# The first modulation of a conditioned decoder block: one sum over 2048 columns, or four groups of 512, and the first products in quarters

## The reference, cut to what matters

```python
def rms_norm(x, g):
    y = x * lax.rsqrt(jnp.mean(x * x, axis=-1, keepdims=True) + EPS)
    return y * g
def modulate(h, shift, scale):
    return h * (1.0 + scale[:, None, :]) + shift[:, None, :]

cond = jax.nn.silu(c)                        # c: (1, 1024)
mod = cond @ w_ada[0] + b_ada[0]             # w_ada: (1024, 9 * 1024)
sh1, sc1, gt1, sh2, sc2, gt2, sh3, sc3, gt3 = jnp.split(mod, 9, axis=-1)
h = modulate(rms_norm(x, g_ffn1), sh1, sc1)  # x: (1, 1024 tokens, 1024)
x = x + 0.5 * gt1 * ((silu(h @ w1_a) * (h @ w3_a)) @ w2_a)     # d_ff = 2816
# ... then a token-mixing layer, a second SwiGLU block, a last rms_norm
```

## Time and profile before

| | |
|---|---|
| median of 3 runs | 2172.11 us (2169.89 to 2172.18) |
| the profiled execution, own time | 2172.18 us |
| its span | 2170.4 us |
| TensorE busy | 2112.2 us, 97% of the span |
| VectorE, ScalarE, GpSimd busy | 1208.2, 697.0, 1256.6 us |
| mean granted TensorE clock | 0.99 of full |

### The profile page before, as it was taken

How to read it: one execution, slowest core, us unless ns; L and a number is a source line. 1 busy time by engine, 2 the same in 40 slices (tenths; PEclk the granted TensorE clock), 3 DMA queues, 4 the chain that set the end, 5 groups by cost and what they waited for, 6 DMA issues and landing times.

```text
span 2170.4 us, 27323 instructions
## 1 busy us (share of the span) xinstructions
PE 2112.2 (97%) x9650; PEld 1735.7 (80%) x9650; DVE 1208.2 (56%) x1293; ACT 697.0 (32%) x1086; POOL 1256.6 (58%) x876
## 2 busy tenths in 40 slices
PE   7999999999999999999999999999999999999998
PEld 5788888888887778787778778887888888888887
DVE  6865445363556787877875753338532333333246
ACT  5633231313223453332332420116321313232234
POOL 1565563737455367867877765544763737464560
PEclk8999999999999999999999999999999999999999
DMA  8132424151421332232335444311111212112111
GB/s 292 59 117 71 143 69 146 58 174 40 139 73 44 122 97 93 79 103 84 97 79 159 144 161 152 107 48 39 49 57 32 59 58 58 58 39 68 32 56 78
DMA packets 228940, 197.04 MB, mean 91 GB/s; under 512 B 17028, under 2 KB 201520, under 8 KB 227696
## 3 DMA queue, kind: packets, MB, share of 16 engines
q1 hardware_dynamic: 204208, 154.42, 23.0%
q10 hardware_dynamic: 24640, 41.40, 5.9%
HBM read 169.45 MB, written 25.17 MB: 90 GB/s over the span
## 4 chain that ended last, share of the span: by engine, by line
PE 83%; DVE 6%; POOL 3%; ACT 2%; DMA 2%; issue 2%; ACTq 1%; SPq 0%; POOLq 0%; DVEq 0%
PE unit_b L1324 10%; PE unit_d L1324 10%; PE unit_c L1118 9%; PE unit_d L1118 9%; PE unit_c L1324 8%; PE unit_a L1324 7%; PE unit_b L1050 7%; PE unit_a L1050 4%; PE unit_a L930 3%; PE unit_b L930 3%; PE unit_c L930 2%; PE unit_d L930 2%; POOL w_low L812 2%; DMA ada_first<-in_w_ada 1%; PE unit_c L1344 1%
## 5 line engine op out<-in xcount | busy, mean ns | idle before, releaser
L861 POOL TENSOR_TENSOR w_low<-raw,w_high 128x512 fp32r<-128x512 f32 x200 | 273.5, 1368 | 214.6 <-ACT w_high L1663 199.1
L831 POOL TENSOR_TENSOR w_low<-raw,w_high 128x512 fp32r<-128x512 f32 x96 | 141.0, 1471 | 287.0 <-ACT w_high L1620 287.0
L1663 ACT ACTIVATE w_high<-raw 128x512 fp32r<-128x512 f32 x200 | 126.5, 632 | 399.8 <-PE unit_b L1324 140.7
L812 POOL TENSOR_TENSOR w_low<-raw,w_high 128x512 fp32r<-128x512 f32 x100 | 152.7, 1527 | 87.6 <-ACT w_high L1845 81.6
L861 POOL TENSOR_TENSOR w_low<-w_mixed,w_high 128x512 fp32r<-128x512 f32 x80 | 107.2, 1340 | 66.2 <-ACT w_high L1663 61.0
L2452 DVE TENSOR_TENSOR fg_two<-fg_one,unit_b 128x512 f32<-128x512 f32 x60 | 41.2, 687 | 168.0 <-PE unit_b L1324 167.8
L779 POOL TENSOR_TENSOR w_high<-raw,ones 128x512 fp32r<-128x512 f32 x44 | 63.0, 1431 | 94.9 <-PE unit_b L930 30.5
L1620 ACT ACTIVATE w_high<-raw 128x512 fp32r<-128x512 f32 x96 | 60.1, 628 | 172.3 <-PE unit_c L1118 67.1
L1845 ACT ACTIVATE w_high<-raw 128x512 fp32r<-128x512 f32 x100 | 61.3, 628 | 151.0 <-PE unit_b L1050 76.9
L2452 DVE TENSOR_TENSOR fg_one<-fg_one,unit_d 128x512 f32<-128x512 f32 x80 | 54.7, 684 | 94.4 <-PE unit_d L1324 94.4
L1050 PE MATMUL unit_b<-t_high,w_high 128*128 128x512 f32 x240 | 94.1, 392 | 6.7 <-POOL w_low L812 6.7
(11 more groups left out here) (530 smaller groups left out, 6152.6 us busy)
## 6 DMA issues: line engine op xcount, KB each, us to landing
raw<-in_w_a SPq DMA_DIRECT2D x66, 512.0 KB, 4.6
raw<-in_w_b SPq DMA_DIRECT2D x66, 512.0 KB, 3.9
raw<-in_w_in SPq DMA_DIRECT2D x44, 512.0 KB, 3.9
ada_ring<-in_w_ada SPq DMA_DIRECT2D x84, 256.0 KB, 3.7
ada_first<-in_w_ada SPq DMA_DIRECT2D x8, 1024.0 KB, 20.9
sg_kept<-s ACTq DMA_DIRECT2D x16, 512.0 KB, 2.7
s<-sg_kept ACTq DMA_DIRECT2D x16, 512.0 KB, 3.4
ada_ring_last<-in_w_ada SPq DMA_DIRECT2D x28, 256.0 KB, 3.5
```

The source lines that it names most:

```text
L812: pool.tensor_tensor(low_, mixer_plain(q, slots), high.bitcast(F32), ALU.subtract).then_inc(mixer.operand_low, 1)
L831: pool.tensor_tensor(low_, plain, high.bitcast(F32), ALU.subtract).then_inc(f.operand_low, 1)
L861: pool.tensor_tensor(low_, weight_plain(PRODUCTS[q][0], slots), high.bitcast(F32), ALU.subtract).then_inc(f.operand_low, 1)
L1663: act.activation(operand((RING[n] + q) % 4)[0], weight_plain(PRODUCTS[q][0], slots), ACT.Copy).then_inc(f.operand_high, 1)
```

## The change

`w_ada`'s first 2048 columns are now taken in four groups (`MOD_GROUPS`), each with the 256 columns of the shift and the 256 of the scale that belong to two channel tiles. Each group is loaded in two halves of the contraction, by two DMAs each (so 16 DMAs of 512 KB with 1 KB in a row). The first tiles of w1 and w3 are loaded between groups 1 and 2. VectorE sums contraction tiles 0 to 6 of a group (512 columns); tile 7 goes to TensorE, which adds it in the products of one column each (`mod_columns`, 4 columns with 2 products each in a group). Groups 0 and 1 are summed before the first reciprocal, groups 2 and 3 between the steps of the norm, two operations after each of the first seven `low`. TensorE makes columns of groups 0 and 1 between the sums of squares of the first and the second half of the tokens, those of groups 2 and 3 before its steps 4 and 8.

The norm and the first two tiles' products go by quarters: step = 4 * quarter + channel tile, with the quarters (first half of the tokens, tiles 0 to 3), (second half, 0 to 3), (first half, 4 to 7), (second half, 4 to 7). The second reciprocal comes after `low(1)` instead of `low(4)`. ScalarE takes the second root before step 4 of its norm instead of ahead of the norm, and its squares start when all of x is copied. ScalarE's waits for `first_mod` stand before steps 0, 2, 8 and 10.

```diff
-FIRST_MOD = ((0, 2), (2, KD))
+MOD_GROUPS = 4
+BY_VECTOR = KD - 1
+BY_PE = tuple(range(BY_VECTOR, KD))
...
         def normed(n, step):
-            return divmod(step, KD)
+            if n > 0:
+                return divmod(step, KD)
+            quarter, k = divmod(step, HK)
+            return quarter % 2, HK * (quarter // 2) + k
...
-            for k in range(KD):
-                sp.dma_start(ada_first[:, k, :], ada[:, k, 0:16 * P]).then_inc(ada_loaded[k], 16)
-            for r, w in enumerate((a["w1_a"][0], a["w3_a"][0])):
-                sp.dma_start(raw[:, r, :, :], ...)
+            for g in range(MOD_GROUPS):
+                for z in range(2):
+                    for kind in range(2):
+                        first = KD * P * kind + 2 * P * g
+                        sp.dma_start(ada_first[g][:, HK * z:HK * z + HK, kind, :],
+                                     ada[:, HK * z:HK * z + HK, first:first + 2 * P]).then_inc(ada_loaded[2 * g + z], 16)
+                if g == 1:
+                    for r, w in enumerate((a["w1_a"][0], a["w3_a"][0])):
+                        sp.dma_start(raw[:, r, :, :], ...)
...
-            take(A_, 1)
-            for half in range(2):
-                for m in range(KD): ... sums of squares ...
+            def mod_columns(g):
+                pe.wait_ge(ada_summed, g + 1)
+                for n in range(4):
+                    tile = slice((n % 2) * P, (n % 2) * P + P)
+                    to = unit[D_][:, HALF * (g % 2) + 4 * g + n:HALF * (g % 2) + 4 * g + n + 1]
+                    last = pe.matmul(to, ada_first_sum[:, g, n * P:n * P + P], ones[:, 0:1], start=True, stop=not BY_PE)
+                    for k in BY_PE:
+                        last = pe.matmul(to, ada_first[g][:, k, n // 2, tile], cond[:, k:k + 1], start=False,
+                                         stop=k == BY_PE[-1])
+                last.then_inc(ada_full, 1)
+
+            take(A_, 1)
+            square_sums(0)
+            take(D_, J // 2)
+            mod_columns(0)
+            mod_columns(1)
+            square_sums(1)
...
-                for half in range(2):
+                for step in range(2 * KD):
+                    half, k = normed(2 * f.n, step)
...
+                    if f.n == 0 and step in (4, 8):
+                        mod_columns(step // 4 + 1)
+                    pe.wait_ge(h_ready, h0 + step + 1)
...
-                    if n > 0 and step == 6:
+                    if step == (4 if n == 0 else 6):
                         root(1)
...
+            def ada_columns(g, k):
+                if k % HK == 0:
+                    dve.wait_ge(ada_loaded[2 * g + k // HK], 32)
+                to = ada_first_sum[:, g, :]
+                from_ = ada_first[g][:, k, :, :].rearrange("p s n -> p (s n)")
+                if k == 0:
+                    last = dve.tensor_scalar(to, from_, cond[:, k:k + 1], None, mul)
+                else:
+                    last = dve.scalar_tensor_tensor(out=to, in0=from_, scalar=cond[:, k:k + 1], in1=to, op0=mul, op1=add)
+                if k == BY_VECTOR - 1:
+                    last.then_inc(ada_summed, 1)
+                else:
+                    own.then(last)
 
             dve.wait_ge(cond_ready, 1)
-            ada_columns(ada_first_sum, ada_first, 16 * P, ada_loaded)
+            for g in range(2):
+                for k in range(BY_VECTOR):
+                    ada_columns(g, k)
             root(0, 0)
...
+            later_columns = [(g, k) for g in (2, 3) for k in range(BY_VECTOR)]
...
-                    if n == 0 and step == 0:
-                        first_mod(0)
+                    if n == 0 and step < 2:
+                        first_mod(step)
                 for step in range(2 * KD):
                     low(step)
...
-                    if step == 1 and n == 0:
-                        first_mod(1)
-                        dve.sem_inc(unit_free[D_], 1)
-                    if step + ahead == KD:
+                    if n == 0:
+                        for g, k in later_columns[2 * step:2 * step + 2]:
+                            ada_columns(g, k)
+                        if step in (5, 8):
+                            first_mod((step + 1) // 3)
+                        if step == 8:
+                            dve.sem_inc(unit_free[D_], 1)
+                    if step + ahead == (HK if n == 0 else KD):
                         root(n, 1)
                     if step + ahead < 2 * KD:
                         scaled(step + ahead)
```

More of the change, by code:

```diff
@@ L312, in block_kernel @@
         x_rows = sb("x_rows", [P, J, D], rH)
-        ada_first = sb("ada_first", [P, KD, 16 * P], rM)
-        ada_first_sum = sb("ada_first_sum", [P, 16 * P], rH + 56 * KB)
+        ada_first = [sb(f"ada_first{g}", [P, KD, 2, 2 * P], rM + 16 * KB * (MOD_GROUPS - 1 - g)) for g in range(MOD_GROUPS)]
+        ada_first_sum = sb("ada_first_sum", [P, MOD_GROUPS, 4 * P], rH + 32 * KB)
         sq = sb("sq", [P, KD, HALF], rA)
@@ L960, in _, with square_sums @@
                 last.then_inc(setup_full, 1)
-            take(A_, 1)
-            for half in range(2):
+            def square_sums(half):
                 for m in range(KD):
@@ L980, in statistics @@
                 pe.matmul(unit[u][:, t], ones[:, :], s0[:, t], start=False, stop=True).then_inc(stat_full, 1)
[L982 to L988, removed]
             def mixer_whole(here, between):
@@ L1545, in _ @@
                     own.then(load_sqrt())
+            for half in range(2):
+                t = slice(HALF * half, HALF * half + HALF)
                 act.wait_ge(unit_free[C_], 2 * half + 2)
@@ L1565, in norm @@
                 if n == 0:
-                    root(1)
                     for o in range(4):
@@ L1582, in norm @@
                     act.wait_ge(xr_done, 2 * KD * n + step + 1)
-                    for part, (k0, _) in enumerate(FIRST_MOD):
-                        if n == 0 and step == k0:
-                            act.wait_ge(mod_done, part + 1)
+                    if n == 0 and half == 0 and m % 2 == 0:
+                        act.wait_ge(mod_done, m // 2 + 1)
                     own.then(act.activation(tile, tile, ACT.Identity, scale=scale[n][:, m:m + 1],
@@ L2154, in derive_scale, with first_mod @@
                                                 in1=vt[:, GN[n] + k0:GN[n] + k1], op0=add, op1=mul)
[L2156 to L2160 removed]
+            later_columns = [(g, k) for g in (2, 3) for k in range(BY_VECTOR)]
+            def first_mod(g):
+                k0, k1 = 2 * g, 2 * g + 2
+                dve.wait_ge(ada_full, g + 1)
+                for n, first in enumerate((SH[0], SC[0])):
                     a0, a1 = first + k0, first + k1
[L2162 to L2163 removed]
+                    at_ = HALF * (g % 2) + 4 * g + 2 * n
+                    own.then(dve.tensor_tensor(mod[:, a0:a1], unit[D_][:, at_:at_ + 2], vt[:, B_ADA + a0:B_ADA + a1], add))
                 derive_scale(0, k0, k1).then_inc(mod_done, 1)
[L2165 removed]
+                dve.wait_ge(mod_done, g + 1)
             def norm(n, h0, end=None, sums=None):
```

67 lines of the change are left out of this document (19 added, 48 removed).

## The result

| | before | after |
|---|---|---|
| median | 2166.14 us (2162.02 to 2172.18, 12 runs) | 2170.23 us (2165.86 to 2178.06, 12 runs) |
| the profiled execution, own time and span | 2172.18, 2170.4 us | 2178.06, 2176.2 us |
| TensorE busy | 2112.2 us | 2117.1 us |

The ratio is 1.0022, 95% interval [1.0012, 1.0033]: 4.8 us slower, between 2.6 and 7.1 (the two medians alone are 4.1 apart). The forecast was 4.9 us slower. But it set this on 2172.18 us, and the kernel before is at 2166.14 when it is measured twelve times; its first three runs lay high. So the 2177.1 us forecast lies 6.9 us above the measured median.

The account below looks back on a forecast made before the run. VectorE, up to the norm's end at 71.4 us, was the bound. Earlier start -8.9, sums in the loop +11.7, stand for columns +2.4, rest -0.3: 2172.18 + 4.9 = 2177.1 us; range 2169 to 2184.

Parts of the forecast that it names:

- The base: Whole kernel: the profiled execution's own 2172.18 us, 0.07 above the median, to which the change of +4.9 us was added.
- Arrival: Loads of the groups: a group's half in 3.0 us at 347 GB/s, landing at 18.9, 21.9, 24.9 and 27.9.
- Sums ahead: VectorE before the first reciprocal: 0.87 us a sum, reciprocal at 30.7 instead of 39.57, a gain of 8.9 us.
- The rival of cheaper sums: VectorE's sums at 0.75 us each, or a shorter stand: +2 us or so, 2174.3 us; chance 0.24.
- the 1.3 us that the prediction set aside for it: Group 1's last sums on VectorE: one could wait for a GpSimd operation, adding up to 1.3 us to the sum.
- Lead in: VectorE from first reciprocal to first `low`: 30.7 + 3.39 + 0.6 + 1.63 + 0.6 + 0.71 + 0.6 = 38.2 us.
- The thin cover: TensorE's second-half sums of squares end at 41 to 42, ScalarE's second root due at 42.5; any lateness is on the path.
- The loop: VectorE's norm steps 0 to 6: 2.94 us each, 11.7 us of sums in them, step 7 begins at 62.4.
- The wait of `first_mod(3)`: VectorE behind `low(8)`: stands 2.4 us, from 64.2 to 66.6, until TensorE has made the last columns.
- The tail: Norm steps 10 to 15 at ScalarE's pace: last low part at 76.3 against 71.4, TensorE's part ends at about 78.
- near 111 of more than 2.3 us: Sign that the forecast is right: TensorE's stand behind the first tiles, now at 106.33 and 2.31 us long, later and longer.
- all behind the norm moves by 4.9: VectorE's later sums, low parts and ring hang on the norm's end and were to move by 4.9 us.

Follow-up runs that it names:

- after_again: The changed kernel once more with no edit, for a second profile; ratio to the kernel before 1.0018.
- sq_split: Against the changed kernel, TensorE makes half of the second half's sums of squares ahead of group 1's columns; ratio to the kernel before 1.0020.
- cols_early: Against the changed kernel, TensorE makes the columns of group 3 before its step 7 instead of step 8; ratio to the kernel before 1.0013.
- split_early: Against the changed kernel, both TensorE moves: second squares split around group 1's columns, group 3's columns before step 7; ratio to the kernel before 1.0005.

## Why the prediction was right or wrong

The direction was right, and the mechanism in its kind: VectorE's sums in the loop take more than the earlier start gives. The size agrees in part by luck, and the absolute time was wrong, because of the base it was added to. The 0.2% taken as the bound between same and slower lies inside the measured interval, so which of the two it is stays undecided by that bound, though slower than before at all is sure.

- **The base, the step that failed.** "The profiled execution's own time is 2172.18, 0.07 above the median: 2172.18 + 4.9 = 2177.1 us." Twelve runs put the kernel before at 2166.14. The median of three said nothing of the spread, and the profile, which could have, was read only up to 110 us. The 4.1 us stand at 671 and the clock behind it were in it; the repeated profile shows that 4.0 us of them come and go, and 2.1 more up to the next stage. With 2166.14 the same sum gives 2171.0, 0.8 above the measured median.
- **Arrival.** A group's half in 3.0 us at an estimated 347 GB/s: the stage from 20 to 24 us shows 348, and the sums start at 18.95, 24.89 (0.62 behind the end of group 0's) and 28.00. w1 and w3 were there at 30.94 and 32.74 (due by 31.7).
- **Sums ahead.** 0.87 a sum was too much, 0.78 to 0.81 measured; the loads set group 1, and the reciprocal started at 30.24 (30.7). The rival of cheaper sums was right on this term. GpSimd did not touch these sums, since it began at 31.72 and they ended at 30.3; so the 1.3 us that the prediction set aside for it did not arise. But it touched two other operations. GpSimd's timeline in the kernel after:

```profile
33.52 3.74 POOL L855 TENSOR_TENSOR w_low<-raw,w_high 128x512 fp32r<-128x512 f32 x3 [0.53 <-ACT w_high L1593]
```

The `low` that VectorE began at 36.68 took 1.12 instead of 0.69 us and ended at 37.80, 0.54 behind the end of GpSimd's row (37.26). In the kernel before, the scale of `first_mod(0)` began at 43.95, took 1.07 us instead of 0.16 to 0.21, and ended at 45.02; GpSimd's row of the same kind ended at 41.28 + 3.72 = 45.00. By the Trainium skill, page "SBUF — State Buffer", section "SBUF: two separate sides", of a VectorE operation on two SBUF inputs and a GpSimd operation that reads SBUF, the one that starts first holds the shared ports for its whole instruction, and the other waits. The trace agrees: both VectorE operations began while GpSimd's ran and ended behind it.
- **Lead in.** First `low` at 38.2 forecast, 36.68 measured; of the 1.5 us, 1.0 is that scale operation, whose 1.63 us for `first_mod(0)` I had carried over from a row with GpSimd beside it.
- **The thin cover.** "Each us more here is a us on the path": this stood in the text as a risk, with the sums of squares done at 41 to 42, and the sum has it at nothing. They were done at 44.0 in one execution and at 40.7 in the other, and the root's stand was 3.05 and 0. This is the term of the sum that was missing.
- **The loop.** 2.94 us a step forecast, 2.76 to 2.78 measured (56.14 to 58.92); 10.2 us for the 14 sums instead of 11.7: the mis-sized term of the sum. `low(7)` came at 62.75, forecast 62.4, as the cheaper sums and the root's stand cancel. In after_again, without that stand, it is 3.2 sooner.
- **The wait of `first_mod(3)`.** 2.4 us forecast, from 64.2 to 66.6; 2.22 measured, from 64.64 to 66.86, and 2.21 and 2.23 in after_again and sq_split. It goes when the columns are made a step sooner (cols_early), as it should.
- **The tail.** Last low part forecast at 76.3, measured 76.56 and 73.3. TensorE's part forecast at 78, measured 78.56. TensorE's stand "near 111 of more than 2.3 us" ended at 110.45 and was 1.81: TensorE was itself 4.6 us late, so there was less to wait for. The date was right, the length wrong, and only the date counts. That all behind the norm moves by 4.9 was too much: 1.0 us was lost in the shorter waits for the loads of `ada_ring`.

So about half of the agreement of +4.9 with +4.8 is luck. At the norm's end the steps came to +5.15 in the first pair of profiles, because the root's stand of 3.05, forecast as nothing, made good the 1.5 us of cheaper sums and the 1.5 of the shorter lead in; in the second pair, without that stand, they came to 2.3, half of the forecast. What the measured 4.8 has beyond that is in part the stand, where it comes, and in part the 2 to 3 us between 705 and 1400 us that no run explains.

## What to carry to other kernels

Starting a stage 9 us sooner gains nothing if the work moved into it is as long: here the loads hid all of VectorE's sums, and the change took 10 us of them out of this cover and put them between the steps of a loop with three engines near their limit. Where engines alternate, removing the work of one shows the next at once; so order the other engine's work first (TensorE's two moves in split_early gave back as much as ten sums left out: ratios 1.0005 and 1.0006). And a forecast of 0.2% needs the kernel's level from many runs: compare the difference with the difference, and look through the whole trace for stands that another execution may lack.

## What the hardware showed beside this

- One program, two executions: 2170.4 and 2164.1 us of span. 6.0 of the 6.3 us come from TensorE's clock behind its stands, from the waits for a few loads, and from one stand at 671 us. In front of that stand VectorE works on small tables, two SBUF inputs of up to 128 columns, beside GpSimd. Four such operations take 5.4 us in the slower execution and 3.15 in the other, which is 2.3 of the 2.5 us by which the stands differ. In the slower one GpSimd's operation began 0.09 us before VectorE's, in the other 0.14 us after it (VectorE and GpSimd, the first profile of before, then the second):

```profile
663.93 2.73 DVE L2309 TENSOR_TENSOR tmp_small<-turn_low 128x128 f32<-128x128 f32 x2
666.69 2.67 DVE L2309 TENSOR_TENSOR turn_low<-tmp_small 128x64 f32<-128x64 f32 x2
663.84 1.30 POOL L855 TENSOR_TENSOR raw<-raw 128x512 f32<-128x512 f32 x1 [0.23 <-POOL w_low L861]
```

```profile
661.63 1.60 DVE L2309 TENSOR_TENSOR tmp_small<-turn_low 128x128 f32<-128x128 f32 x2
663.26 1.52 DVE L2309 TENSOR_TENSOR turn_low<-tmp_small 128x64 f32<-128x64 f32 x2
661.77 1.31 POOL L855 TENSOR_TENSOR raw<-raw 128x512 f32<-128x512 f32 x1 [0.23 <-POOL w_low L861]
```

- A short stand of TensorE could cost more than its own length, by the clock behind it: products of 512 columns followed each other by 0.43 instead of 0.23 us, and one-column pairs were 0.56 instead of 0.36 long. The length of the stand alone does not decide. Behind one of 2.04 us (after_again, 107.43) the granted clock was 1.00 until 111. Behind one of 1.81 (after, 110.45) it was 1.00 for 1.2 us and then 0.51 for 3.2, and so it was behind one of 2.31 (before, 106.33). Behind one of 2.82 (after, 49.55) it was 0.95 for 0.8 us and 0.51 from 50.3 to 53.7. Behind those of 2.89, 2.91 and 4.08 the products went at half clock at once.
- Short sums are dearer by column: 0.78 us for 512 columns, 2.48 for 2048, so 0.62 for each 512 in the long one.
